# Rotations of the query heads split between ScalarE and VectorE, an earlier second score, and the samples' first loads in three portions on SyncE

## What is computed

```python
c, kr = rms_norm(x @ w_dkv[:, :256]), rope(x @ w_dkv[:, 256:])   # keys and values shared by all heads
cq = rms_norm(x @ w_in[:, :512]); gate = x @ w_in[:, 512:]
q = cq @ w_uq                         # per head: 128 plain elements + 64 that are rotated
q_lat, q_rope = q[:128] @ w_uk, rope(q[128:])
s = (q_lat @ c.T + q_rope @ kr.T) * 192 ** -0.5     # masked by chunks of 64 frames
o = softmax(s) @ c @ w_uv
out = (o * silu(gate)) @ w_out
```

## Time and profile before

| | |
|---|---|
| median of 3 executions | 2070.52 us (2070.36 to 2072.48) |
| the profiled execution | 2070.16 us, its span 2067.7 us |
| mean granted TensorE clock | 0.978 of 2.4 GHz |
| TensorE busy | 94% of the span |
| VectorE, ScalarE, GpSimd busy | 54%, 35%, 23% |

### The profile page before, as it was taken

One profiled execution on the slowest core, in us unless ns is written; L12 is line 12 of the kernel. 1 busy time (PEld: TensorE's weight loads), 2 busy tenths in 40 slices (PEclk: granted clock), 3 DMA queues, 4 the chain that ended last, 5 costly groups with the idle time before them and its releaser, 6 DMA issues.

```text
span 2067.7 us, 31546 instructions
## 1 busy us (share of the span) xinstructions
PE 1940.8 (94%) x11755; PEld 1826.6 (88%) x11755; DVE 1123.3 (54%) x1964; ACT 719.6 (35%) x1247; POOL 467.5 (23%) x390
## 2 busy tenths in 40 slices
PE   7999999999869999999899999999999869999997
PEld 6999999999758899999898988988988759988886
DVE  3365545645657512422467766666677447763643
ACT  3333233323231121211354444453443347762100
POOL 0121122212212110000244444443444410000111
PEclk9999999999989999999999999999999979999999
DMA  5121122211173212233111111111111233364421
GB/s 162 42 74 49 37 73 63 63 32 55 34 256 122 74 51 66 81 116 109 54 32 50 38 55 46 39 53 52 36 46 37 78 86 86 92 213 151 138 92 41
DMA packets 190337, 158.78 MB, mean 77 GB/s; under 512 B 36176, under 2 KB 174928, under 8 KB 190000
## 3 DMA queue, kind: packets, MB, share of 16 engines
q1 hardware_dynamic: 176608, 131.49, 20.7%
q10 hardware_dynamic: 13184, 24.69, 3.7%
q0 software_dynamic: 464, 1.48, 0.2%
HBM read 115.78 MB, written 41.84 MB: 76 GB/s over the span
## 4 chain that ended last, share of the span: by engine, by line
PE 50%; DVE 8%; issue 6%; ACT 4%; POOL 2%; ACTq 1%; DMA 1%; DVEq 0%; SPq 0%; POOLq 0%
PE ps L118 15%; PE ps L120 15%; PE ps L119 15%; POOL h_p L1608 2%; PE ps L1721 2%; DVE h_mx L1933 1%; DVE h_p L1892 1%; PE ps L1703 1%; PE ps L1704 1%; ACT h_p L1825 1%; DVE s_mx L2497 1%; DVE h_pt_l L112 1%; ACTq L2116 1%; DVE h_v_l L112 1%; DVE h_kt_l L112 0%
## 5 line engine op out<-in xcount | busy, mean ns | idle before, releaser
L1617 POOL TENSOR_SCALAR h_p<-h_p,h_rsum 128x128 f32<-128x128 f32 (+7 forms) x128 | 220.7, 1726 | 305.9 <-DVE h_rsum L1937 305.8
L118 PE MATMUL a_pj<-act_h,a_w_l 128*128 128x384 f32 x768 | 276.6, 360 | 7.3 <-DVE act_l L112 7.3
L120 PE MATMUL a_pj<-act_h,a_w_h 128*128 128x384 f32 x768 | 261.1, 340 | 0.0
L119 PE MATMUL a_pj<-act_l,a_w_h 128*128 128x384 f32 x768 | 261.1, 340 | 0.0
L1825 ACT ACTIVATE h_p<-ps,h_mx 128x128 f32<-128x128 f32 (+7 forms) x128 | 95.1, 743 | 235.6 <-DVE h_mx L1933 208.8
L112 DVE TENSOR_TENSOR h_pt_l<-ps,h_pt_h 128x128 fp32r<-128x128 f32 (+2 forms) x192 | 100.3, 553 | 130.5 <-ACT h_pt_h L107 128.9
L118 PE MATMUL ps<-act_h,m_c_l 128*128 128x384 f32 x480 | 163.7, 341 | 4.1 <-DVE act_l L112 2.4
L119 PE MATMUL ps<-act_l,m_c_h 128*128 128x384 f32 x480 | 163.2, 340 | 0.0
L120 PE MATMUL ps<-act_h,m_c_h 128*128 128x384 f32 x480 | 163.1, 340 | 0.0
L118 PEld LDWEIGHTS a_pj<-act_h,a_w_l 128*128 128x128 f32 x768 | 145.4, 189 | 12.6 <-DVE act_l L112 8.0
L119 PEld LDWEIGHTS a_pj<-act_l,a_w_h 128*128 128x128 f32 x768 | 145.6, 190 | 3.4 <-issue 3.4
(11 more groups left out here) (325 smaller groups left out, 4956.1 us busy)
## 6 DMA issues: line engine op xcount, KB each, us to landing
a_w_raw<-in_w_in_a SPq DMA_DIRECT2D x32, 512.0 KB, 4.1
m_c_raw<-in_w_in_b SPq DMA_DIRECT2D x20, 512.0 KB, 4.2
scratch_gate<-m_sg SPq DMA_DIRECT2D x16, 576.0 KB, 5.2
h_gate<-scratch_gate SPq DMA_DIRECT2D x64, 128.0 KB, 2.0
scratch_og<-h_gate SPq DMA_DIRECT2D x64, 128.0 KB, 1.7
o_w_raw<-in_w_out_b SPq DMA_DIRECT2D x16, 512.0 KB, 7.7
o_g_raw<-scratch_og SPq DMA_DIRECT2D x24, 256.0 KB, 4.0
a_factors<-in_x SPq DMA_DIRECT2D x9, 512.0 KB, 5.5
```

The costliest lines, as they stand in the source:

```text
L118: nc.tensor.matmul(out, ll, rh, start=first, stop=False)
L119: nc.tensor.matmul(out, lh, rl, start=False, stop=False)
L120: return nc.tensor.matmul(out, lh, rh, start=False, stop=last)
L1617: nc.gpsimd.tensor_scalar(weights_of(u), weights_of(u), rsum[:, u % PB], None, ALU.mult).then_inc(S["p_ready"], 1)
```

## The change

Four edits.

1. **Who rotates.** VectorE keeps the product with the cosines (`cosines`). ScalarE then copies the four quarters out of PSUM to their turned places (`shift`), VectorE multiplies all 128 partitions with a sine table whose signs are exchanged accordingly, and adds both heads itself (`sines`). GpSimd takes no part. The parts lie at three places of `p`, the third at its end.
2. **The order at the seam of two pairs.** Scores 1 and `exp` 1 stand behind V1, no more behind V3; `exp` 0, 1 and 3 wait for the low part of the first, second and third rotation. ScalarE shifts R0 and R1 in units 14 and 15, VectorE does `sines` 0 and `gated` G6 ahead of `turned` 15, and the third rotation's `sines` behind G7.
3. **The order inside a pair.** For even units ScalarE does `turned(u)` and the next unit's projection ahead of `exp(u+3)`; for odd ones VectorE does the reciprocal behind the projection.
4. **The samples' first loads** are issued by SyncE: sample 0's keys behind G1's store of the last pair, all queries behind G3's, sample 1's keys behind G5's. GpSimd zeroes the loads' ends behind unit 6, the keys' ends behind unit 9.

```diff
@@ constants
-    c["sin_t"] = np.concatenate([sin.T, -sin.T] * 2, 0)
+    c["sin_t"] = np.concatenate([-sin.T, sin.T] * 2, 0)
@@ parts
-        at = (tg % 2) * 4 * TG + i * TG
+        at = (0, 3 * TG, PB * SEQ - 3 * TG)[tg] + i * TG
@@ SyncE
-                if g == 2:
+                if g == (1 if last else 2):
                     sp.wait_ge(S["proj_out"], pr * NP + NP)
...
+                    if last:
+                        k.samples.load_first_keys(sp)
+                if last and g == 3:
+                    sp.wait_ge(S["ql_stored"], 16 * PAIRS)
+                    sp.wait_ge(S["qr_stored"], 16 * PAIRS)
+                    k.samples.load_queries(sp)
+                if last and g == 5:
+                    k.samples.load_second_keys(sp)
@@ GpSimd
-        rope_adds(0, True)
...
-                if last and u == 8:
+                if last and u == 6:
                     pool.wait_ge(S["proj_out"], PAIRS * NP)
-                    k.samples.zero_first(pool)
-            if not last:
-                rope_adds(pr + 1, False)
+                    k.samples.zero_loads(pool)
+                if last and u == 9:
+                    k.samples.zero_keys(pool)
@@ TensorE
-            for s in ("V1", "V2", "V3"):
+            proj(pr, "V1", first)
+            scores(pr, 1)
+            for s in ("V2", "V3"):
                 proj(pr, s, first)
-            scores(pr, 1)
             scores(pr, 2)
@@ ScalarE
+        def shift(pr, tg, first):
+            act.wait_ge(S["rope_cos"], pr * 3 + tg + 1)
+            x = bank[:, place(f"R{tg}", first), 0:TG]
+            for a, b in ((0, 32), (32, 0), (64, 96), (96, 64)):
+                last = nc.scalar.copy(rope_part(tg, 1)[b:b + 32], x[a:a + 32])
+            last.then_inc(S["rope_moved"], 1)
...
-            if u == 0:
-                act.wait_ge(S["rq_out"], pr * 3 + 3)
+            if u in (0, 1, 3):
+                act.wait_ge(S["rq_out"], pr * 3 + (1, 2, 3)[min(u, 2)])
...
             for s in ("UT", "V0", "R2"):
                 proj(pr, s, first)
             exp(pr, 0)
-            for s in ("V1", "V2", "V3"):
+            proj(pr, "V1", first)
+            exp(pr, 1)
+            for s in ("V2", "V3"):
                 proj(pr, s, first)
-            exp(pr, 1)
-            exp(pr, 2)
             for u in range(UNITS):
...
+                if u % 2 == 0:
+                    beside(u)
+                    if u == 0:
+                        exp(pr, 2)
...
-                if u + 3 < UNITS:
+                if u % 2 and u + 3 < UNITS:
                     exp(pr, u + 3)
                 turned(pr, u)
-                if last and u == 10:
-                    act.wait_ge(S["ql_stored"], 16 * PAIRS)
-                    act.wait_ge(S["qr_stored"], 16 * PAIRS)
-                    k.samples.load_first(act)
+                if u % 2 == 0:
+                    beside(u + 1)
+                    if u + 3 < UNITS:
+                        exp(pr, u + 3)
+                if u >= UNITS - 2 and not last:
+                    shift(pr + 1, u - UNITS + 2, False)
             if not last:
-                for s in ("R0", "R1"):
-                    proj(pr + 1, s, False)
+                proj(pr + 1, "R0", False)
+                proj(pr + 1, "R1", False)
+                shift(pr + 1, 2, False)
@@ VectorE
-        def rope(pr, tg, first):
...
+        def cosines(pr, tg, first):
...
+            nc.vector.tensor_tensor(rope_part(tg, 0), x, cos[:, tg * TG:tg * TG + TG], ALU.mult).then_inc(S["rope_cos"], 1)
+        def sines(pr, tg):
+            dve.wait_ge(S["rope_moved"], pr * 3 + tg + 1)
             dve.sem_inc(S["proj_out"], 1)
+            x = rope_part(tg, 1)
+            nc.vector.tensor_tensor(x, x, sin[:, tg * TG:tg * TG + TG], ALU.mult).then_inc(S["rope_sin"], 1)
+            dve.wait_ge(S["rope_cos"], pr * 3 + tg + 1)
+            dve.wait_ge(S["rope_sin"], pr * 3 + tg + 1)
+            for e in range(2):
+                rows = slice(e * RD, (e + 1) * RD)
+                done = nc.vector.tensor_tensor(rope_sums(tg)[:, e], rope_part(tg, 0)[rows], x[rows], ALU.add)
+            done.then_inc(S["rope_sum"], 1)
...
             largest(pr, 0)
+            proj(pr, "V1", first)
+            largest(pr, 1)
+            proj(pr, "V2", first)
+            inverted(pr, 0)
+            proj(pr, "V3", first)
             rope_low(pr, 2)
-            for s in ("V1", "V2", "V3"):
-                proj(pr, s, first)
-            inverted(pr, 0)
-            largest(pr, 1)
             inverted(pr, 1)
             largest(pr, 2)
...
-                if u + 2 < UNITS:
+                if u % 2 == 0 and 0 < u and u + 2 < UNITS:
                     inverted(pr, u + 2)
...
+                if (u % 2 or u == 0) and u + 2 < UNITS:
+                    inverted(pr, u + 2)
...
+                if u == UNITS - 1:
+                    if not last:
+                        sines(pr + 1, 0)
+                    gated(pr, NG - 2)
                 turned(pr, u)
-            gated(pr, NG - 2)
             if not last:
-                rope(pr + 1, 1, False)
-                rope_third(pr + 1, False)
+                sines(pr + 1, 1)
+                cosines(pr + 1, 2, False)
+                rope_low(pr + 1, 0)
                 rope_low(pr + 1, 1)
+                gated(pr, NG - 1)
+                sines(pr + 1, 2)
```

More of the change, by code:

```diff
@@ L1494, in heads_programs @@
     bank = k.bank
-    names = ("uq_loaded ukv_loaded zeroed wh_ready wl_ready table_loaded proj_done proj_high proj_out rope_step rope_sum rq_high rq_out s_done masked max_done "
+    names = ("uq_loaded ukv_loaded zeroed wh_ready wl_ready table_loaded proj_done proj_high proj_out rope_cos rope_moved rope_sin rope_sum rq_high rq_out s_done masked max_done "
              "exp_done inv_done scale_go p_ready t_done t_high t_out pv_done o_out ql_stored qr_stored qs_ready").split()
@@ L1598, in _ @@
     def _(pool):
-        def rope_adds(pr, first):
-            for tg in range(NTG):
-                pool.wait_ge(S["rope_step"], pr * 3 + tg + 1)
-                if tg == 0 and not first:
-                    pool.wait_ge(S["p_ready"], pr * UNITS)
-                for e in range(2):
-                    rows = slice(e * RD, (e + 1) * RD)
-                    done = nc.gpsimd.tensor_tensor(rope_sums(tg)[:, e], rope_part(tg, 0)[rows], rope_part(tg, 1)[rows], ALU.add)
-                done.then_inc(S["rope_sum"], 1)
-        rope_adds(0, True)
         def body(pr, first, last):
@@ L1843, in _, with beside @@
             nc.scalar.activation(x[:, 0, 0:P], k.ident[:], ACT.Identity, scale=0.0).then_inc(S["zeroed"], 1)
-        for s in ("R0", "R1"):
-            proj(0, s, True)
+        shift(0, 0, True)
+        shift(0, 1, True)
+        proj(0, "R0", True)
+        proj(0, "R1", True)
+        shift(0, 2, True)
         def body(pr, first, last):
+            def beside(u):
+                if u in BESIDE and BESIDE[u][0][0] != "R" and not (last and BESIDE[u][1]):
+                    s, n = BESIDE[u]
+                    proj(pr + n, s, first and not n)
             for s in ("UT", "V0", "R2"):
@@ L1850, in body @@
             exp(pr, 0)
-            for s in ("V1", "V2", "V3"):
+            proj(pr, "V1", first)
+            exp(pr, 1)
+            for s in ("V2", "V3"):
                 proj(pr, s, first)
-            exp(pr, 1)
-            exp(pr, 2)
             for u in range(UNITS):
-                if u in BESIDE and BESIDE[u][0][0] != "R" and not (last and BESIDE[u][1]):
-                    s, n = BESIDE[u]
-                    proj(pr + n, s, first and not n)
+                if u % 2 == 0:
+                    beside(u)
+                    if u == 0:
+                        exp(pr, 2)
                 if u in SPLITS and not last:
@@ L1955, in _ @@
         dve.wait_ge(S["table_loaded"], 32)
-        rope(0, 0, True)
-        rope(0, 1, True)
-        def rope_third(pr, first):
-            rope_low(pr, 0)
-            dve.wait_ge(S["rq_out"], pr * 3 + 1)
-            rope(pr, 2, first)
-        rope_third(0, True)
+        cosines(0, 0, True)
+        cosines(0, 1, True)
+        sines(0, 0)
+        sines(0, 1)
+        cosines(0, 2, True)
+        rope_low(0, 0)
         rope_low(0, 1)
+        sines(0, 2)
         def body(pr, first, last):
@@ L1983, in body @@
                     s, n = BESIDE[u]
-                    if s == "R0":
-                        rope(pr + 1, 0, False)
-                    elif s[0] != "R":
+                    if s[0] == "R":
+                        cosines(pr + 1, int(s[1]), False)
+                    else:
                         proj(pr + n, s, first and not n)
+                if (u % 2 or u == 0) and u + 2 < UNITS:
+                    inverted(pr, u + 2)
                 if u + 3 < UNITS:
@@ L2003, in body @@
                 k.samples.first_keys_low(dve)
-            gated(pr, NG - 1)
+                gated(pr, NG - 1)
         pairs(dve, body)
```

(11 more changed lines are left out.)

12 lines of the change are left out of this document (2 added, 10 removed).

## The result

| | before | after |
|---|---|---|
| median | 2070.44 us (2069.90 to 2072.48, 4 executions) | 2014.81 us (2013.77 to 2017.45, 4 executions) |
| ratio | | 0.9731 (95% interval 0.9715 to 0.9748) |
| profiled execution, span | 2070.16, 2067.7 us | 2017.45, 2015.5 us |
| granted TensorE clock | 0.978 | 0.983 |

The change makes the kernel 55.6 us faster by the medians. The forecast was 2023, 47 us faster, in a range of 2011 to 2041.

What follows compares the result with a forecast made beforehand. TensorE, busy 94% of the span, was taken to set the time. Seams and clocks 25.5 us, pair 0 4 us and the last pair 17.4 us sum to 47 us off 2070.2, forecast 2023 us, range 2011 to 2041.

Steps and rivals of the forecast that it cites:

- What bounds the kernel: Whole kernel: TensorE, busy 94% of the span, sets the time; a pair can give back 4.6 us at most.
- The copies and sums: Rotation: a quarter's copy on ScalarE takes 0.5 us, VectorE's sine product and each sum 0.56, low parts 0.95.
- The seam, 25.5 us: Seams between pairs: 3.4 us at each of 7 seams, 24 us, with two lowered clocks of 0.9 us less.
- All four waits: TensorE's seam waits: 0.51 us for turned weights, 0.56 and 2.14 for `exp` 0 and 1, 0.47 for KB0's low part.
- the 0.3 us left for VectorE's backlog: Each seam: 0.3 us of the 3.7 kept back for low parts of V2, V3, KB0 behind one another.
- The order inside the pair counts as nothing: Inside a pair: later `exp(u+3)` and earlier `turned` gain nothing; without cover, a cost of 1 us at every even unit.
- Pair 0, 4 us: Pair 0: scores 0 stay, waits of 1.42 and 2.14 us go, a new one of about 0.9 comes; 4 us gained.
- The last pair, 17.4 us: Last pair: moving the issues off ScalarE gives 20.1 us, net 17.4 after later GpSimd scaling and turned 15.
- GpSimd's wait: Last pair: GpSimd waits for QL behind unit 6, so turn 7 starts 2.4 us late, of which 1.5 charged.
- Turned 15 behind gated G6: Last pair: this order puts the low parts of sample 0's keys 1.2 us behind their readers.
- The rule on issuing engines: Last pair: by this rule moving the issues would give next to nothing, sum near 2041; the prediction held the trace disagrees.
- The slower rival: Seam: ScalarE's quarter copies become the chain, eating the 47 us from 1.15 us a copy; 2085 at 1.3 us; chance 0.04.

Runs made afterwards that it cites:

- exp0_waits_third: Changed kernel with `exp` 0 waiting for the low part of the third rotation again: 2012.32 us.
- loads_on_scalar: Changed kernel with all fourteen of the samples' first load issues on ScalarE again, in one go behind unit 10: 2036.32 us.
- the mend: Changed kernel with zeroing behind unit 7, last pair's turned 15 ahead of gated G6, pair 0's first low part before the third cosines: 2011.41 us.
- The dose: Changed kernel with each quarter copied by ScalarE in four pieces of 96 columns, 16 copies a rotation for 4: 2031.31 us.
- one_portion: Changed kernel with queries and both samples' keys issued by SyncE in one portion behind G1's store: 2023.71 us.

## Why the prediction was right, and where it was short

**What bounds the kernel**: right. TensorE's work is the floor, and the pairs went down to it: TensorE is busy for all but 0.5 of 77.0 us.

**The copies and sums**: right in size. A quarter takes 0.47 us (0.5 taken), a sine product or sum 0.55 (0.56), the low parts 0.95 each. ScalarE starts `exp` 0 at the end of the third rounding and `exp` 1 ends at 1181.9, 2.4 us ahead of scores 3 (1.9 forecast).

**The seam, 25.5 us**: too small. All four waits went, so the 0.3 us left for VectorE's backlog was not due.

**"The order inside the pair counts as nothing"**: this step failed. It read only what the new order delays, not what it brings forward. The wait of 0.61 us for KA0's low part stood in every pair's timeline before, and the new order rounds KA0 ahead of an `exp`. It is worth 0.65 us a pair. With the 0.3 us of reserve this is 1.0 of the 1.2 us a pair by which pairs 1 to 6 (29.3 us, where six seams at 3.4 and the clocks made 22) went beyond the sum. The rest, about 0.2 us, I cannot place; TensorE's busy time in a pair fell from 77.0 to 76.5, and matmul ends are modelled.

**Pair 0, 4 us**: measured 4.8. Of these 0.34 us belong to the seam at its end and 0.60 to its own wait for KA0's low part, which leaves 3.9. Scores 0 did not stay where they were: they wait 2.25 us for 1.91. The new wait for V0's low part, 0.9 in the working, is 1.5 to 1.6 us where the clock stays up (exp0_waits_third) and 0.4 or nothing where it has fallen and V1 itself takes longer (the run with the later zeroing, the changed kernel).

**The last pair, 17.4 us**: right in its main term and in its sum, the latter in part by luck. 21.1 us less 3.2 for its entry is 17.9. The issues were the wait, as `loads_on_scalar` shows, and 1.66 us are left of it where 2.3 were forecast. GpSimd's wait was forecast as 2.4 us late, 1.5 charged: 1.97 us waited and, with the clock, 2.8 us lost, 1.1 where the clock stays up. Turned 15 behind gated G6 was charged 1.2 us: the mend won 0.2 and left the wait of 0.75 us, so this charge was wrong. The errors of about 1 us each cancel. SyncE's six issues took the 5.7 us assumed, and G6's gate came in time by less than a microsecond.

**The rule on issuing engines.** The Trainium skill ("DMA: Bandwidth & Descriptors", "Issuing engines are not separate DMA queues") has it that spreading issues saves only sequencer time, usually small. Its first half agrees with the runs: the transfers took about as long from either engine (the queries landed 9.1 us after their issue from ScalarE, 9.8 us from SyncE). The second does not: fourteen issues in one go hold a sequencer for 20.3 to 20.5 us, on ScalarE and on SyncE, and where they stand is worth 16 to 21 us, their portions 8. In three portions they take 12.2 us in all.

**The slower rival** was said to start where a copy takes 1.15 us, from 1.9 us of slack ahead of `exp` 1. The dose and the quarters on VectorE show that the thin place is another one: V0's low part, which ended at 1177.70 us, just as V1 did on TensorE, ahead of scores 1. Copies 0.16 us longer each already cost 1.7 us a pair, and the kernel that lengthened VectorE's list there by 5 us lost all that the seams had given and most of the last pair's gain. My working had the two within half a microsecond of each other and did not read that as the limit.

**Why the median fell 8 us below the forecast** (2023 against 2014.8): about 7 us from pairs 1 to 6, the rest from pair 0 and the last pair (0.5 us each).

## What to carry to other kernels

When a chain runs through several engines, the worth of a move is not a property of the move: price it with the other moves made and unmade, since whichever link is shorter shows no gain. Look in the timeline for every wait of the bounding engine, also those that an edit seems only to touch in passing, and ask of a new order both what gets late and what gets early. DMA issues belong on the sequencer whose next work has the most slack, in portions small enough for what stands behind them. Before a stage's microsecond is put down to an edit, compare the granted clock of the two stages.

## What was not expected of the hardware

- A DMA's cost on the issuing engine depends on what is under way. The same rows of 16 KB and 4 KB, issued behind 2.5 MB of queries and 1 MB of keys, hold ScalarE for 4.15 and 4.66 us (`loads_on_scalar`) and SyncE for 4.23 and 4.87 us (`one_portion`); issued behind the 1 MB of keys without the queries they take 0.61 and 1.13 us on SyncE (the changed kernel). The second copy of the 4 KB row takes 2.5 us in the one case and 2.3 in the other.
- The duration of a short ScalarE copy is not its price in a row of them: 32x96 takes 0.229 us, but sixteen take 2.58 us, 0.16 each, while 32x384 takes 0.47 us and four take 1.92. So cutting a copy in four doubles the summed durations and lengthens the stretch by a third.
- A wait of 3.4 us costs more than itself: with the quarters on VectorE the two waits of a seam are 4.9 us, and the pair is 6.9 us longer, with the granted clock at 0.65 in the 3 us around the end of such a wait.
- A wait of 1.98 us does not always bring the clock down: behind the same wait it was 0.76 for 7 us in six profiled executions and 1.00 in five.
